# Prompt attention: the value product by single heads, high and low parts side by side

## What is computed

```
p = softmax(q k^T * scale + mask)          # 1024 x 1024 a head, lower triangle
o = p v                                    # 1024 x 64 a head
```

## Time and profile before

| what | value |
|---|---|
| median of 3 runs | 1721.24 us (1719.73 to 1721.5) |
| span of the profiled execution, first to last instruction | 1725.7 us |
| mean granted TensorE clock | 0.965 of full |
| the two attention stages in that span | about 276 to 878 us |

### The profile page before, as it was taken

How to read it: one execution, slowest core, us unless ns; L and a number is a source line. 1 busy time by engine, 2 the same in 40 slices (tenths; PEclk the granted TensorE clock), 3 DMA queues, 4 the chain that set the end, 5 groups by cost and what they waited for, 6 DMA issues and landing times. The chain is left out here.

```text
span 1725.7 us, 29397 instructions
## 1 busy us (share of the span) xinstructions
PE 1625.7 (94%) x10253; PEld 1461.3 (85%) x10253; DVE 1128.5 (65%) x1953; ACT 779.4 (45%) x1628; POOL 887.1 (51%) x781
## 2 busy tenths in 40 slices
PE   7999978999998799999989979999999999999997
PEld 6778867888887688888878779999999999888876
DVE  6533334767775667676643686775777776799886
ACT  5312214666676566666532243333333333433354
POOL 1000002656565278776830387776777775344464
PEclk9999995999999899999999989999999999999999
DMA  8366645232320856655576526566666665965532
GB/s 270 125 185 236 215 133 141 52 102 59 93 65 24 202 170 183 171 161 149 168 233 179 189 65 200 184 175 193 197 190 195 192 191 162 371 236 170 176 119 92
DMA packets 218160, 285.10 MB, mean 165 GB/s; under 512 B 36009, under 2 KB 140586, under 8 KB 212860
## 3 DMA queue, kind: packets, MB, share of 16 engines
q1 hardware_dynamic: 218018, 283.27, 54.1%
HBM read 235.66 MB, written 114.41 MB: 203 GB/s over the span
## 5 line engine op out<-in xcount | busy, mean ns | idle before, releaser
L2481 POOL TENSOR_TENSOR lead<-acc,lead 128x512 fp32r<-128x512 f32 x110 | 147.2, 1347 | 107.4 <-ACT lead L2613 107.4
L1112 POOL TENSOR_SCALAR a_pr<-a_pr,a_rden 128x256 f32<-128x256 f32 (+7 forms) x128 | 94.4, 749 | 197.7 <-DVE a_rden L1212 193.0
L817 PE MATMUL zp<-win_h,xT_h 128*128 128x512 f32 (+1 forms) x288 | 113.0, 393 | 3.3 <-DVE acc L668 3.3
L817 PE MATMUL zp<-win_l,xT_h 128*128 128x512 f32 (+1 forms) x288 | 111.8, 388 | 0.0
L2613 ACT CAST lead<-acc 128x512 fp32r<-128x512 f32 x105 | 64.9, 620 | 101.0 <-PE z_ps L3139 61.0
L1153 ACT ACTIVATE a_pr<-a_pr,a_nm 128x256 f32<-128x256 f32 (+7 forms) x128 | 98.6, 772 | 22.0 <-DVE a_nm L1206 21.3
L2671 ACT CAST lead<-d_ring 128x512 fp32r<-128x512 f32 x73 | 45.4, 622 | 127.8 <-PE r_ps L3231 26.9
L1286 PE MATMUL a_o<-a_ph,a_vh 128*128 128x256 f32 x288 | 88.3, 307 | 12.6 <-DVE a_pl L1216 12.5
L817 PE MATMUL zp<-win_h,xT_l 128*128 128x512 f32 (+1 forms) x256 | 99.6, 389 | 0.0
L2552 POOL TENSOR_TENSOR u_op<-d_w,u_op 128x512 fp32r<-128x512 f32 x39 | 54.7, 1406 | 78.0 <-ACT u_op L2683 78.0
L2481 POOL TENSOR_TENSOR u_op<-acc,u_op 128x512 fp32r<-128x512 f32 x44 | 80.5, 1832 | 8.9 <-DVE o_tl L2829 8.9
(11 more groups left out here) (438 smaller groups left out, 5435.1 us busy)
## 6 DMA issues: line engine op xcount, KB each, us to landing
out_s_win_k<-in_state_win_k SPq DMA_DIRECT2D x40, 816.0 KB
out_s_win_v<-in_state_win_v SPq DMA_DIRECT2D x40, 816.0 KB
d_ring<-scratch_s_a SPq DMA_DIRECT2D x106, 256.0 KB, 3.1
acc<-in_state_win_k SPq DMA_DIRECT2D x16, 768.0 KB, 6.1
acc<-in_state_win_v SPq DMA_DIRECT2D x16, 768.0 KB, 5.7
scratch_s_a<-u_us SPq DMA_DIRECT2D x22, 544.0 KB, 5.9
acc<-in_w_gate SPq DMA_DIRECT2D x23, 512.0 KB, 9.0
acc<-in_w_up SPq DMA_DIRECT2D x22, 512.0 KB, 11.3
```

What stands on the lines that cost most here:

```text
L817: last = nc.tensor.matmul(z[:, 0:n], a, b, start=(k == 0 and i == 0), stop=(k == KC - 1 and i == len(terms) - 1))
L1112: nc.gpsimd.tensor_scalar(p, p, self.rden[:, k % 2, h:h + 1], 1.0, ALU.mult, ALU.mult)\
L2481: nc.gpsimd.tensor_tensor(op[n][:, 1, :], src, op[n][:, 0, :].bitcast(F32), ALU.subtract).then_inc(S["lo"], 1)
```

## The change

The matmuls of `value` take one head each. The weights are 128 columns that hold vh and vl of this one head (`vv`, for head 1 with vl first), and the moving operand is 256 columns that hold ph and pl of this head (`pp`). So one matmul makes vh ph, vh pl, vl ph and vl pl of a head. There are two matmuls per key block, one a head, where there were three. `o_bank` grows to a full bank, 128 x (2 x 256). What `out` does changes:

- DVE: two `tensor_reduce` from PSUM, one a head, each 64 partitions, adding vh ph and vh pl (256 elements in, 128 out) into `ot`
- ACT: waits for both, then two copies of 64 x 128, one a head, of vl ph from PSUM to the other 64 partitions of `cross`, a piece of `pr` that the steps don't use
- POOL: a new `out` event, `ot` = `ot` + `cross`, 128 x 128, after both; `store` waits for it.

```diff
-        self.vh = [sb(t(f"vh{i}"), [P, PT, 2 * HD], F32R) for i in range(2)]
-        self.vl = [sb(t(f"vl{i}"), [P, PT, 2 * HD], F32R) for i in range(2)]
-        self.ph, self.pl = (sb(t(n), [P, PT, 2, P], F32R) for n in ("ph", "pl"))
+        self.vv = [sb(t(f"vv{i}"), [P, PT, 4 * HD], F32R) for i in range(2)]
+        self.vh = [v[:].rearrange("p j (a c) -> p j a c", a=4)[:, :, 0:4:3] for v in self.vv]
+        self.vl = [v[:].rearrange("p j (a c) -> p j a c", a=4)[:, :, 1:3] for v in self.vv]
+        self.pp = sb(t("pp"), [P, PT, 2, 2, P], F32R)
+        self.ph, self.pl = (self.pp[:, :, :, i] for i in range(2))
...
+        self.cross = [self.pr[:, 0, i, SEQ - P:] for i in range(2)]
...
-        self.o_bank = ps(t("o"), [P, 2, P])
+        self.o_bank = ps(t("o"), [P, 2, 2 * P])
...
-            E.append((("value", k), 0.36 * (s + 1)))
+            E.append((("value", k), 0.24 * (s + 1)))
...
         elif what == "store":
...
-            sp.wait_ge(S["o_a"], n * PT + 4 * f + 4)
-            sp.wait_ge(S["o_d"], n * PT + 4 * f + 4)
+            sp.wait_ge(S["o_sum"], n * PT + 4 * f + 4)
...
     def gpsimd(self, pool, e):
...
+        elif e[0] == "out":
+            k = e[1]
+            out = self.ot[:, k % PT * P:(k % PT + 1) * P]
+            pool.wait_ge(S["o_a"], 2 * k + 2)
+            pool.wait_ge(S["o_d"], 2 * k + 2)
+            nc.gpsimd.tensor_tensor(out, out, self.cross[k % 2], ALU.add).then_inc(S["o_sum"], 1)
...
     def scalar(self, act, e):
...
             act.wait_ge(S["o_ps"], k + 1)
-            if s % 4 == 0 and n:
-                act.wait_ge(S[f"o_out{s // 4}"], 16 * n)
-            nc.scalar.copy(self.ot[0:HD, s * P:(s + 1) * P], self.o_bank[0:HD, 0, :]).then_inc(S["o_a"], 1)
+            act.wait_ge(S["o_d"], 2 * k + 2)
+            if k >= 2:
+                act.wait_ge(S["o_sum"], k - 1)
+            for h in range(2):
+                to, of = (slice(x * HD, (x + 1) * HD) for x in (h, 1 - h))
+                nc.scalar.copy(self.cross[k % 2][to], self.o_bank[of, h, 0:P]).then_inc(S["o_a"], 1)
...
     def vector(self, dve, e):
...
-            nc.vector.tensor_copy(self.ot[HD:P, s * P:(s + 1) * P], self.o_bank[HD:P, 1, :]).then_inc(S["o_d"], 1)
+            for h in range(2):
+                r = slice(h * HD, (h + 1) * HD)
+                nc.vector.tensor_reduce(self.ot[r, s * P:(s + 1) * P], self.o_bank[r, h].rearrange("p (a q) -> p q a", a=2),
+                                        AX.X, ALU.add).then_inc(S["o_d"], 1)
...
     def tensor(self, pe, e):
...
             if k:
-                pe.wait_ge(S["o_a"], k)
-                pe.wait_ge(S["o_d"], k)
+                pe.wait_ge(S["o_a"], 2 * k)
+                pe.wait_ge(S["o_d"], 2 * k)
...
-                    for i, (x, y) in enumerate(((vh, self.ph), (vh, self.pl), (vl, self.ph))):
-                        last = nc.tensor.matmul(self.o_bank[:], x[:, kb, :], y[:, kb], start=(kb == 0 and i == 0),
-                                                stop=(kb == s and i == 2))
+                    for h in range(2):
+                        last = nc.tensor.matmul(self.o_bank[:, h], self.vv[n % 2][:, kb, h * P:(h + 1) * P],
+                                                self.pp[:, kb, h].rearrange("p a q -> p (a q)"),
+                                                start=(kb == 0 and h == 0), stop=(kb == s), skip_group_check=True)
...
 LATENT_LATER = {
+    "gpsimd": {(0, "out"): 5},
...
 DILATED_LATER = {
-    "gpsimd": {(1, "v_split"): -18},
+    "gpsimd": {(0, "out"): 5, (1, "v_split"): -18},
...
 class WindowSide:
...
-                      (0.008, ("load_v", 1)), (0.028, ("pre",)), (0.030, ("q_block", 0)), (0.032, ("q_block", 1)),
+                      (0.008, ("load_v", 1)), (0.022, ("pre",)), (0.024, ("q_block", 0)), (0.026, ("q_block", 1)),
```

More of the change, by code:

```diff
@@ L956, in __init__ @@
         self.rden = sb(t("rden"), [P, 2, 2])
-        self.o_bank = ps(t("o"), [P, 2, P])
+        self.o_bank = ps(t("o"), [P, 2, 2 * P])
         self.S = {n: sem(t(n)) for n in (
-            "table1 q_in0 q_in1 k_in0 k_in1 v_in k_lo k_ok v_hi v_lo neg_go exp recip norm o_ps o_a o_d o_out0 o_out1 sink").split()}
+            "table1 q_in0 q_in1 k_in0 k_in1 v_in k_lo k_ok v_hi v_lo neg_go exp recip norm o_ps o_a o_d o_sum o_out0 o_out1 sink").split()}
         self.S["table0"] = self.early.sem["causal_in"]
@@ L1119, in gpsimd @@
             vh, vl = self.vh[n % 2], self.vl[n % 2]
-            nc.gpsimd.tensor_scalar(vh[:], self.vn[:], 1.0, 1.0, ALU.mult, ALU.mult).then_inc(S["v_hi"], 1)
+            v = self.vn[:].rearrange("p j (a c) -> p j a c", a=2)
+            nc.gpsimd.tensor_scalar(vh, v, 1.0, 1.0, ALU.mult, ALU.mult).then_inc(S["v_hi"], 1)
             pool.wait_ge(S["v_hi"], n + 1)
-            nc.gpsimd.tensor_tensor(vl[:], self.vn[:], vh[:].bitcast(F32), ALU.subtract).then_inc(S["v_lo"], 1)
+            nc.gpsimd.tensor_tensor(vl, v, vh.bitcast(F32), ALU.subtract).then_inc(S["v_lo"], 1)
+        elif e[0] == "out":
[4 more added lines that the diff above has]
+            nc.gpsimd.tensor_tensor(out, out, self.cross[k % 2], ALU.add).then_inc(S["o_sum"], 1)
     def scalar(self, act, e):
@@ L1278, in tensor @@
             if k:
-                pe.wait_ge(S["o_a"], k)
-                pe.wait_ge(S["o_d"], k)
-            vh, vl = self.vh[n % 2], self.vl[n % 2]
+                pe.wait_ge(S["o_a"], 2 * k)
+                pe.wait_ge(S["o_d"], 2 * k)
             for u in range(self.units[s]):
```

## The result

The change makes the kernel slower: 1765.48 us (median of 4 runs, 1743.75 to 1767.48) against 1720.49 us, a ratio of 1.0223 (95% interval 1.017 to 1.0276), some 38 us by the ratio and 45 by the medians. Its four runs spread by 24 us. The prediction was 1697 us, range 1686 to 1717.

A forecast was written before the change was run, and what follows sets the result against it. PE, busy 94% in both attention stages, was taken as the bound. The terms -35 + 7 + 2 + 2 = -24 us took a profiled 1725.7 us to 1701.7, and the median to 1697 us, range 1686 to 1717.

The forecast's parts named there:

- The first term, -35 us: PE's value product: 288 matmuls removed at 0.12 us from start to start, plus 0.6 us at half clock; -35 us.
- even the short half is PE's: Short steps of a pair: PE busy all of 24.7 us, DVE 79%, so time taken from PE should come back.
- The order: unknown within some 3 us either way; zero.: Plan's weight 0.24 for 0.36 and earlier window-side events: they move events and add none; zero, within some 3 us.
- POOL: nothing, with 3 us as the upper end.: POOL's new add, 0.46 us a step, 29 us in all, in an engine with slack; nothing, 3 us upper end.
- a load ahead: SP's page and window loads behind the store come at most a couple of us later, into buffers already one load ahead.
- +2 us for the release and ACT.: PE's next product waiting for the bank and ACT waiting for DVE's reduces: +2 us together, 0 and 8 as ends.
- has four to ten us: Between two products PE has four to ten us of transposes, scores and sample work, so little of ACT's delay arrives.
- DVE's reduces, +7 us: DVE's two reduces for one copy, 0.42 us each, 35 us of work; +7 us reaches PE, 0 and 20 as ends.
- The two ends, +2 us: Ends of both stages, where nothing hides the chain: 0.55 us later after stage 0, 1.5 after stage 1; +2 us.
- The slower rival: Waits on the bank ahead of `value` and on DVE ahead of ACT's casts show every step; 1746 us, chance 0.11.
- The clock: Rival: a relieved PE has more holes, so half-clock stretches multiply; 12 us more, 1709 us, chance 0.08.
- the prediction's own sign of being wrong: Wrong if PE's waits naming DVE or ACT grow by over 20 us, or the stages' clock falls below 0.93.

The follow-up runs named there:

- product_alone: Kernel before with the new matmuls only: old plan, old `out` (one copy each on ACT and DVE), two cross terms missing in the output; 1704.08 us, 0.988.
- filler: Changed kernel with as many matmuls as the change removed put back ahead of each product, their result overwritten; 1772.34 us, 1.0307.
- order_only: Kernel before with only the plan's new numbers: value weight 0.24 for 0.36 and three earlier window-side events; 1743.09 us, 1.0124.
- order_back: Changed kernel with value's weight back at 0.36 and the three early window-side events at their old places; 1735.24 us, 1.0085.
- store_late: Changed kernel with the store event 24 places later in SP's order, so window and page loads go ahead of it; 1741.11 us, 1.0128.
- both_act_late: Changed kernel with old weights and early places, SP's store 24 places later, and ACT's `out` six places later in stage 1; 1716.21 us, 0.9968.
- clean: Changed kernel with old weights and places, store 24 places later, no ACT copies or POOL add, reduces kept (vl ph missing); 1700.14 us, 0.9881.
- both: Changed kernel with old weights and early places and SP's store 24 places later; 1724.2 us, 1.0013.

## Why the prediction was wrong, point by point

The sum failed in four terms: the gain was taken whole (-35, measured -21), and three costs stood at nothing or nearly so: the order (0, measured some 21 to 24), the store behind POOL's add (0, some 16), and ACT's copies with the casts behind them (+2 with the release, some 23).

- **The first term, -35 us.** 576 matmuls were left, at 0.12 us from start to start where the clock is full, so the work did leave PE. Its worth was 21 us (`product_alone`), and the interval leaves 35 out. The step that failed is "even the short half is PE's, so time taken from PE's queue should come back as time": it took PE's busy 94% for a bound with nothing close behind it. In the changed kernel only 7 to 14 of 35 us of such work lie on the path (`filler`).
- **"The order: unknown within some 3 us either way; zero."** With ACT's part this was the worst term: some 21 us (`order_only`), 24 by `order_back` against the changed kernel. The sum counted the instructions that an edit adds, but the price lies in when each engine comes to them. Why the new order is worse (tables of shifts by number of places, kept from the old one) is argued, not shown.
- **"POOL: nothing, with 3 us as the upper end."** Mis-sized by the store behind it: some 16 us (`store_late`). The prediction named SP's loads behind the store and gave them "a load ahead"; the rows show SP silent for 22 us and PE idle for the keys. POOL's slack of 193 us said nothing, since at the place shown the add came behind splits of 6.8 us.
- **"+2 us for the release and ACT."** The direct wait on the bank was right, 1.2 us. But ACT's and POOL's part of `out` costs some 23 us with order and store mended. The prediction had the place (stage 1, no shift for ACT's `out`, casts behind it) and priced it at next to nothing, for two reasons. ACT was to stand for the two reduces at most, 0.84 us; it stood up to 6.2 us, because the reduces stand behind other work of DVE. And PE "has four to ten us" of other work between two products; still DVE's wait for the casts grew, and the product's wait for DVE with it. `both_act_late` gives 8 us of it back.
- **DVE's reduces, +7 us.** 0.42 us each as taken. `clean` equals `product_alone`, so they are hidden as far as these runs tell; a cost of 7 us lies within their noise. The Trainium skill (VectorE: DVE Perf Modes, rules for kernel authors) calls this operation DVE's slowest. Here it took 419 ns for 256 elements read from PSUM, about what the subtraction takes that reads as many (415); no run has it as the upper end.
- **The two ends, +2 us.** Right in kind. After stage 1 PE was idle 5.1 us where it was 2.3, some 3 us instead of 1.5; after stage 0, 2.9 for 2.1.
- **The rivals.** The slower rival (1746, chance 0.11) is the nearest. It named ACT's wait ahead of the casts, which was there, but its price came from the bank at every step, which was not (1.2 us), and it had neither the order nor the store; that its number comes within 20 us is luck. The clock was an amplifier: it fell from 0.96 to 0.90 in stage 1, and the prediction's own sign of being wrong, a stage clock below 0.93, was met. The Trainium skill (TensorE: Matmul & The Clock Gate, HAM oscillation) ties low clock to gaps of PE, and the trace agrees in part: 51 us idle there for 26, but in `order_back` 46 us idle at 0.95.

From kernel to kernel the way is: 21 us gained (`product_alone`), nothing for the reduces (`clean`), 23 lost by ACT's and POOL's part (`both`), 36 by order and store together (the changed kernel), 38 in all. These steps must add up, since each starts where the last ends. Only the 36 can be split in two ways: the store costs 12 us where the order is the old one and 16 where it is the new, the order 20 where the store is late and 24 where it is not. Open are why the product alone brings 21 us and not 35, and by which waits the order costs.

A version that beats both kernels came out, by little: old weights and early places, store 24 places later, ACT's `out` six places later in stage 1 (`both_act_late`, 0.3%, the interval just clear of 1 in both series).

## What to carry to other kernels

An engine that is busy 94% need not be a bound that gives back all that leaves it, and it stays one only as long as the queues that feed it keep their places: before pricing what leaves it, walk each queue that a new wait enters and ask what stands behind it, transfer queues first. Changing a planner's numbers is a change of its own, with a price to be tested alone on the old kernel; retuning the shifts after it is the next thing to try. And a run that puts the removed work back as filler tells in one step how much of such work is still on the path.

## What was not expected of the hardware

In the changed kernel, an equal number of matmuls put back cost 7 to 14 us for 35 us of work, and the granted clock of the stages rose with them from 0.91 and 0.90 to 0.94 and 0.92. The reduce reading two runs 128 elements apart in PSUM took about what the subtraction with as many elements from PSUM takes (419 and 415 ns for 256 elements a partition). And the granted clock did not follow PE's idle time alone: in stage 1 it was 0.90 with 51 us idle (the changed kernel), 0.95 with 46 (`order_back`) and 0.96 with 26 and 29 (the kernel before and `order_only`). These are single executions each.
